# Moving the second projection of an attention tile forward in TensorE's order

## What is computed

```
dq, dk, dv = parts of rms_norm(x) @ w_in            # per head: 2x128, 2x128, 256 columns
dq = rope(rms_norm(dq));  dk = rope(rms_norm(dk))
s  = q @ k.T * DK**-0.5                             # one score matrix for each of two maps
p  = softmax(s, masked by chunk);  a = p[map 0] - lam * p[map 1]
o_d = rms_norm(a @ v)
```

## Time and profile before

| | us |
|---|---|
| median of 3 runs | 2159.15 (2158.52 to 2160.07) |
| the profiled execution | 2156.74 |
| its span, first to last instruction | 2155.0 |
| TensorE busy in it | 2143.0 (99%) |
| VectorE busy | 1157.1 (54%) |
| ScalarE busy | 841.6 (39%) |
| mean granted TensorE clock | 0.998 of 2.4 GHz |

### The profile page before, as it was taken

One profiled execution on the slowest core, in us unless ns is written; L12 is line 12 of the kernel. 1 busy time (PEld: TensorE's weight loads), 2 busy tenths in 40 slices (PEclk: granted clock), 3 DMA queues, 4 the chain that ended last, 5 costly groups with the idle time before them and its releaser, 6 DMA issues.

```text
span 2155.0 us, 34904 instructions
## 1 busy us (share of the span) xinstructions
PE 2143.0 (99%) x13462; PEld 2026.1 (94%) x13462; DVE 1157.1 (54%) x2348; ACT 841.6 (39%) x1945; POOL 526.7 (24%) x288
## 2 busy tenths in 40 slices
PE   9999999999999999999999999999999999999999
PEld 9999877789899898998999999999999999999999
DVE  6211544456636556356135648888988972322432
ACT  5200333335556566465312124444344333434411
POOL 5422201230040400501350510000000036576520
PEclk9999999999999999999999999999999999999999
DMA  8522223230040310402952421222222257666211
GB/s 272 193 90 89 62 68 102 78 107 25 27 124 30 89 58 29 120 28 68 322 158 69 149 89 42 80 79 71 90 80 70 80 177 245 199 182 193 88 43 51
DMA packets 319908, 227.19 MB, mean 105 GB/s; under 512 B 17401, under 2 KB 310891, under 8 KB 319756
## 3 DMA queue, kind: packets, MB, share of 16 engines
q1 hardware_dynamic: 223562, 121.66, 19.4%
q10 hardware_dynamic: 96194, 103.48, 14.3%
HBM read 164.47 MB, written 60.62 MB: 104 GB/s over the span
## 4 chain that ended last, share of the span: by engine, by line
PE 98%; DVE 1%; DMA 1%; ACT 0%; issue 0%; ACTq 0%; DVEq 0%
PE ps L832 28%; PE ps L833 28%; PE ps L834 28%; PE ps L1120 3%; PE ps L1096 3%; PE ps L973 1%; PE ps L972 1%; PE ps L1111 1%; PE ps L1043 1%; PE ps L1048 1%; PE ps L1256 1%; PE ps L1045 1%; PE ps L1061 0%; PE ps L1272 0%; PE ps L1027 0%; PE ps L1018 0%
## 5 line engine op out<-in xcount | busy, mean ns | idle before, releaser
L832 PE MATMUL ps<-a_hi,w_all 128*128 128x352 f32 (+1 forms) x1360 | 415.8, 306 | 4.6 <-DVE a_lo L2666 4.6
L834 PE MATMUL ps<-a_hi,w_all 128*128 128x352 f32 (+1 forms) x1360 | 413.7, 304 | 0.0
L832 PE MATMUL ps<-a_hi,w_hi 128*128 128x352 f32 x1240 | 405.6, 327 | 0.0
L834 PE MATMUL ps<-a_hi,w_lo 128*128 128x352 f32 x1240 | 397.5, 321 | 0.0
L833 PE MATMUL ps<-a_lo,w_hi 128*128 128x352 f32 x1240 | 397.4, 320 | 0.0
L833 PE MATMUL ps<-a_lo,w_all 128*128 128x352 f32 (+1 forms) x1200 | 368.6, 307 | 0.0
L734 POOL TENSOR_SCALAR w_hi<-w_raw 128x1024 fp32r<-128x1024 f32 x92 | 101.1, 1099 | 966.6 <-DVE scr L2328 447.2
L832 PE MATMUL ps<-w_hi,a_hi 128*128 128x384 f32 (+1 forms) x768 | 286.4, 373 | 0.0
L834 PE MATMUL ps<-w_hi,a_lo 128*128 128x384 f32 (+1 forms) x768 | 273.4, 356 | 0.0
L833 PE MATMUL ps<-w_lo,a_hi 128*128 128x384 f32 (+1 forms) x768 | 272.8, 355 | 0.0
L832 PEld LDWEIGHTS ps<-a_hi,w_all 128*128 128x128 f32 x1360 | 256.2, 188 | 5.5 <-DVE a_lo L2666 5.2
(11 more groups left out here) (283 smaller groups left out, 3580.2 us busy)
## 6 DMA issues: line engine op xcount, KB each, us to landing
w_raw<-w_in SPq DMA_DIRECT2D x64, 512.0 KB, 4.3
w_raw<-w_down SPq DMA_DIRECT2D x48, 512.0 KB, 3.7
raw_half<-w_up SPq DMA_DIRECT2D x80, 256.0 KB, 3.0
hid_d<-scr ACTq DMA_DIRECT2D x22, 512.0 KB, 2.7
w_raw<-w_down SPq DMA_DIRECT2D x24, 384.0 KB, 3.3
scr<-gates_d ACTq DMA_DIRECT2D x24, 352.0 KB, 6.2
gates_d<-full ACTq DMA_DIRECT2D x13, 528.0 KB, 2.6
xt_d<-full ACTq DMA_DIRECT2D x1, 4224.0 KB
```

Of the source, the lines that this page charges most:

```text
L832: pe.matmul(out, lhs[0], rhs[0], start=start, stop=False)
L834: return pe.matmul(out, lhs[1], rhs[0], start=False, stop=stop)
```

## The change

Part B of the tile `now` is issued straight behind the rest of A, with the waits that stood before it. The first product with v (5) and the second map's scores (6) come behind it. Nothing is added or removed.

```
                 if now:
                     h, i, n = now
                     project(2 * (i % 2), i, PA_SLOT, PA_SLOT + 3, k0=EARLY).then_inc(S["pa_done"], 1)
+                if now:
+                    h, i, n = now
+                    if i == 0:
+                        pe.wait_ge(S["w_split"], 8 * h + (U_DIFF + 7))
+                        if h:
+                            wait_piece(pe, h - 1, 3, S["gate_ev"])
+                        else:
+                            pe.wait_ge(S["gate_ev"], GATE_PIECES)
+                    if n == 1:
+                        pe.wait_ge(S["ot_ev"], RET_TILES)
+                    project(2 * (i % 2) + 1, i, PB_SLOT, PB_SLOT + 3).then_inc(S["pb_done"], 1)
                 if fill:
                     h, k = fill
...
                     scores(1, i).then_inc(S["s1_done"], 1)
-                if now:
-                    h, i, n = now
-                    if i == 0:
-                        pe.wait_ge(S["w_split"], 8 * h + (U_DIFF + 7))
-                        if h:
-                            wait_piece(pe, h - 1, 3, S["gate_ev"])
-                        else:
-                            pe.wait_ge(S["gate_ev"], GATE_PIECES)
-                    if n == 1:
-                        pe.wait_ge(S["ot_ev"], RET_TILES)
-                    project(2 * (i % 2) + 1, i, PB_SLOT, PB_SLOT + 3).then_inc(S["pb_done"], 1)
                 if fill:
                     h, k = fill
                     gate_fill(h, 2 * k + 1)
```

## The result

The changed kernel takes 2186.45 us, median of 4 runs (2185.43 to 2189.84), against 2159.61 for the kernel before (4 runs): a ratio of 1.0124, 95% interval 1.0111 to 1.0136. The profiled execution took 2186.36 us with a span of 2184.6, 29.6 more than before. That is more than the 26.8 between the medians, because the profiled execution before (2156.74 us) was shorter than its kernel's median (2159.61) and this one lies at its own.

A forecast was written before the change was run, and what follows sets the result against it. TensorE was taken as the bound, busy 140.00 of 140.00 us a head; stalls of 2.58 + 2.09 + 1.89 + 0.20 = 6.76 us, times 4 heads = 27.0, on 2159.15 gave 2186.2 us, with an 8-in-10 range of 2175 to 2199.

The forecast's parts named there:

- Tile 4: Step scoring tile 4: the next first scores wait for the copies of q and k, 2.09 us a head.
- Tile 5: Step scoring tile 5: transposes wait for bank 4's copy (1.62 us), next first scores for q and k; 2.58 us in all.
- Tile 6: Step scoring tile 6: the q and k transposes wait for the copy out of bank 4, 1.89 us a head.
- Tile 7: Step scoring tile 7, order unchanged: second scores wait for the first map's exponential, 0.20 us a head.
- Tiles 0 to 3: Steps scoring these tiles: q and k are copied ahead of the weighted difference, just in time; 0 us lost.
- it is not given back later: Behind attention TensorE is again full and what is prepared for it moves along, so the 27.0 us stay lost.
- The thin margins break: Rival: short-tile steps also wait about 0.5 us, or the rotation is late; 8 us more, 2194 us; chance 0.09.
- Only the copy out of bank 4 counts: Rival: q and k come in time, leaving 1.62 and 1.89 us a head; 14 us, 2173 us; chance 0.05.
- Faster by fewer switches: Rival: part A runs into part B without a matmul-kind switch; at most 4.8 us saved, 2154.4 us; chance 0.02.
- Nothing happens: Rival: the lost cover is not needed, as other engines work closer to TensorE; 2159 us; chance 0.03.
- The clock falls as well: Rival: each of 12 long stalls also lowers TensorE's clock, 2.3 us each; 28 us more, 2214 us; chance 0.06.
- The two large waits: Sign in the waits list: L2438 ahead of L1256 (1.6, 1.9 us), L2349 ahead of L1096 (2.1, 0.9 us), eight times each.

The follow-up runs named there:

- e4: The changed kernel, with VectorE copying q and k ahead of the weighted difference for every tile: ratio 1.0064 to the kernel before.
- e5: The changed kernel, with VectorE's copy out of bank 4 ahead of its wait for the second scores: ratio 1.0139 to the kernel before.
- e7: The changed kernel, with 21 instead of 9 of part A's matmuls ahead of the first scores (EARLY = 7): ratio 1.0072 to the kernel before.
- e1: The kernel before, with part B moved forward only in the steps that score tiles 0 to 3: ratio 1.0013 to the kernel before.
- e10: The changed kernel unchanged, run and profiled a second time: ratio 1.0136 to the kernel before.
- e6: The changed kernel, with VectorE's copy out of bank 4 before its second-scores wait and q and k copied before the weighted difference: ratio 1.0072 to the kernel before.
- e2: The kernel before, with part B moved forward only in the steps that score tiles 4 to 6: ratio 1.0117 to the kernel before.
- e3: Against the kernel before, part B moved ahead of the second map's scores only, staying behind the first product with v: ratio 1.0140.

## Why the prediction was right, step by step

**The sum.** Predicted were 27.0 us of stalls and 2186.2 us; measured 26.6 us in the stage (less the clock) and a median of 2186.45. The stalls agree by mechanism. That the medians agree to 0.3 us is partly luck: the profiled execution has 1.7 us of clock and 1.8 behind the stage on top, and executions of one kernel differ by 1.6 (before) and 4.4 us (changed). From the timeline above, by the prediction's own method, with the unhindered start taken from this head's second scores:

- *Tile 4, 2.09 predicted.* Transposes at 693.26, plus 2.23 is 695.49; first scores at 697.49: 2.00.
- *Tile 5, 2.58 predicted, 1.62 of it at the transposes.* Second scores at 707.98, plus 1.30 is 709.28; transposes at 710.97: 1.69. First scores due at 709.28 + 2.13 = 711.41, started 713.87: 2.46.
- *Tile 6, 1.89 predicted.* Second scores at 722.40, plus 1.51 is 723.91; transposes at 725.86: 1.95.
- *Tile 7, 0.20 predicted.* 735.90 against 729.33 + 6.47: 0.10.
- *Tiles 0 to 3, nothing predicted.* Neither of the two waits stands in their steps, and from 637 to 692 TensorE is busy 55.00 of 55 us.

That is 6.51 us a head, 26.0 for four. It is more than the 5.74 us of idle time, as each step loses 0.1 to 0.35 us more than TensorE idles in it: tile 4 loses 2.00 and idles 1.83, tile 5 loses 2.46 and idles 1.53 and 0.58. The matmuls behind a wait have longer records (four of the next first scores take 1.56 us, before 1.45), which count as busy. The remaining 0.6 of the 26.6 is not traced. Among the waits of weight loads, the transposes of the weights of shorter tiles wait 0.6 us a head for the difference (twice), before 0.2 (once); whether that is part of it is not shown.

**That both waits matter, and overlap**, was the argument for each tile taking the larger of two. e4, e5 and e7 remove one each and bear that out. **That nothing in the short steps is lost** held in the full change, and e1 shows how near a wait is. **That it is not given back later** held: behind the stage the spans differ by 1.8 us (1.1 in e10), the wrong way. The prediction had named a change of ConvFFN's length as a sign against it; of the 1.8, TensorE's waits for L2666 have 0.8 (5.4 us against 4.6), the rest is open.

**The rivals.** *The thin margins break*: out for the change, as nothing idles in the steps of tiles 0 to 3. *Only the copy out of bank 4 counts*: out, by e4. *Faster by fewer switches*: no trace of it; without the stalls the stage is not shorter. *Nothing happens*: out. *The clock falls as well* was partly right. I had priced it as every stall or none. It fell behind one stall of twelve in the profiled execution, 1.7 us instead of 28. The sentence that the clock stays at 1.00 there failed, though the time hardly moved. By the Trainium skill (TensorE: Matmul & The Clock Gate, section on a second failure mode, depth-cycling through PSUM) frequent short idle times between groups of matmuls can make the clock swing. The profiles here show single falls behind stalls of about 2 us (four in sixty), and no swing.

**What the page was to show.** The two large waits came at the lines named, eight times each, and a little shorter: 1.53 and 1.80 us for L2438 (1.6 and 1.9 predicted), 1.83 and 0.58 for L2349 (2.1 and 0.9). The wait for L1746 stands only among the weight loads (0.7 us, four times). The idle time of a head is 5.74 us and not 6.8, mostly for the longer records above. One sign failed: TensorE's share of the chain that ended last was to fall by a good 1%, and it fell from 98% to 93%. Five per cent are some 109 us, against 29.6 lost. The chain follows what released TensorE, and behind a stall that leads through work on VectorE (3%) and ScalarE (1%) that ran while TensorE was busy too. The share in that chain is no measure of the time lost.

## What to carry to other kernels

On an engine that is never idle, an order is worth what it covers: before moving independent work, name the chain that runs on the other engines behind it, and take its length less the cover that is left. Here two waits overlapped, so removing the first was worth 0.3 us and the second 11; and half of the cover did five sixths of the work. A stall closed in one step can reappear in the next as a wait on another engine (e6), and an order mixed by step can open one (e1), so follow the second step too.

## What the runs showed of the hardware

A stall of TensorE of 1.8 us (2.15 us between weight loads) can be followed by a stretch at 1.2 GHz (a clock of 0.50 from 551 to 553 in the changed kernel), and mostly is not. The five profiles that have twelve stalls each (the change, e2, e3, e5, e10) show idle times of 1.4 to 2.3 us; tile 5's is split into 1.5 and 0.6 in all but e5. The clock fell behind four of these sixty stalls, three of tile 4 (1.83 us) and one of tile 5 (2.29 us, e5), each time for 1.7 us of loss. In one pair of executions of the same program (the change and e10) the same instruction behind the same 1.83 us was followed by a clock of 0.68 and of 1.00, and that is the whole difference of 1.7 us between their stages. Such a loss is best taken out window by window before two kernels are compared.
